# Two attention pipelines: values before the turn on TensorE, reading them out before the copy on VectorE, with a few edits around them

## The reference

```python
def diff_attend(q, k, v, lam):
    s = jnp.einsum('bqhmd,bkhmd->bhmqk', q, k).astype(jnp.float32) * (HEAD_DIM ** -0.5)
    p = jax.nn.softmax(s, axis=-1)
    w = p[:, :, 0] - lam * p[:, :, 1]
    return jnp.einsum('bhqk,bkhe->bqhe', w.astype(v.dtype), v)
```

## Time and profile before

| | |
|---|---|
| median of 3 runs | 2604.9 us (2600.58 to 2605.96) |
| profiled execution | 2598.19 us, of which its span 2596.4 us |
| TensorE, VectorE, ScalarE busy | 96%, 52%, 40% of the span |
| mean granted clock of TensorE | 0.987 of full |
| first attention pipeline (ab) | 1249 to 1366 us |
| second attention pipeline (cd) | 2270 to 2365 us |
| last product's end to span's end | 2587.5 to 2596.4 us |

### The profile page before, as it was taken

How to read it: one execution, slowest core, us unless ns; L and a number is a source line. 1 busy time by engine, 2 the same in 40 slices (tenths; PEclk the granted TensorE clock), 3 DMA queues, 4 the chain that set the end, 5 groups by cost and what they waited for, 6 DMA issues and landing times.

```text
span 2596.4 us, 37247 instructions
## 1 busy us (share of the span) xinstructions
PE 2490.1 (96%) x15710; PEld 2157.3 (83%) x15710; DVE 1350.2 (52%) x2245; ACT 1035.2 (40%) x1659; POOL 0.2 (0%) x4
## 2 busy tenths in 40 slices
PE   7999999999999999999789999999999999988998
PEld 6998789978997888888568888888888887868998
DVE  6657554655453334357886333335333347846554
ACT  5534544434433223146563322213222226744442
POOL 0000000000000000000000000000000000000000
PEclk9999999999999999999999999999999999999999
DMA  9886733488862333335102323332333326502554
GB/s 334 283 277 207 234 122 98 145 321 302 311 211 90 97 98 98 97 122 186 41 1 66 103 96 96 96 97 90 97 97 97 98 89 181 184 1 67 185 180 137
DMA packets 145639, 372.28 MB, mean 143 GB/s; under 512 B 20266, under 2 KB 65730, under 8 KB 145474
## 3 DMA queue, kind: packets, MB, share of 16 engines
q1 hardware_dynamic: 145186, 369.59, 44.0%
q10 hardware_dynamic: 288, 0.31, 0.1%
HBM read 368.71 MB, written 1.15 MB: 142 GB/s over the span
## 4 chain that ended last, share of the span: by engine, by line
PE 88%; DVE 7%; ACT 3%; issue 1%; DMA 1%; SPq 0%; ACTq 0%; DVEq 0%
PE psum L352 76%; PE psum L834 2%; PE psum L1701 2%; PE psum L1672 1%; DVE normed_raw L618 1%; DVE normed_lo L631 1%; PE psum L1689 1%; PE psum L1603 1%; PE psum L1291 1%; PE psum L1303 1%; DVE weights_lo L300 1%; DVE arena L1768 0%; ACT arena L1721 0%; PE psum L1166 0%; PE psum L1275 0%
## 5 line engine op out<-in xcount | busy, mean ns | idle before, releaser
L300 DVE TENSOR_TENSOR weights_lo<-weights_raw,weights_hi 128x1024 fp32r<-128x1024 f32 (+2 forms) x547 | 656.9, 1212 | 471.8 <-ACT weights_hi L294 469.0
L352 PE MATMUL psum<-normed_hi,weights_hi 128*128 128x256 f32 (+2 forms) x2664 | 880.6, 331 | 21.6 <-DVE normed_lo L631 6.8
L352 PE MATMUL psum<-normed_lo,weights_hi 128*128 128x256 f32 (+2 forms) x2664 | 866.7, 325 | 0.0
L352 PE MATMUL psum<-normed_hi,weights_lo 128*128 128x256 f32 (+2 forms) x2664 | 866.3, 325 | 0.0
L294 ACT CAST weights_hi<-weights_raw 128x1024 fp32r<-128x1024 f32 (+2 forms) x547 | 562.8, 1035 | 371.8 <-DMA weights_raw<-in_w_down 260.9
L352 PEld LDWEIGHTS psum<-normed_hi,weights_hi 128*128 128x128 f32 (+1 forms) x2664 | 508.6, 191 | 85.5 <-issue 35.1
L352 PEld LDWEIGHTS psum<-normed_lo,weights_hi 128*128 128x128 f32 (+1 forms) x2664 | 509.8, 191 | 41.5 <-issue 1.2
L352 PEld LDWEIGHTS psum<-normed_hi,weights_lo 128*128 128x128 f32 (+1 forms) x2664 | 509.6, 191 | 40.6
L352 PE MATMUL psum<-hidden_hi,weights_hi 128*128 128x512 f32 (+1 forms) x594 | 217.6, 366 | 0.0
L352 PE MATMUL psum<-hidden_hi,weights_lo 128*128 128x512 f32 (+1 forms) x594 | 217.1, 365 | 0.0
L352 PE MATMUL psum<-hidden_lo,weights_hi 128*128 128x512 f32 (+1 forms) x594 | 217.1, 365 | 0.0
(11 more groups left out here) (264 smaller groups left out, 2740.3 us busy)
## 6 DMA issues: line engine op xcount, KB each, us to landing
weights_raw<-in_w_gu SPq DMA_DIRECT2D x220, 512.0 KB, 3.6
weights_raw<-in_w_down SPq DMA_DIRECT2D x110, 512.0 KB, 3.6
arena<-in_w_mod SPq DMA_DIRECT2D x72, 512.0 KB, 6.9
weights_raw<-in_w_x SPq DMA_DIRECT2D x24, 512.0 KB, 6.5
resid<-in_w_mod SPq DMA_DIRECT2D x24, 512.0 KB, 7.5
normed_raw<-in_w_mod SPq DMA_DIRECT2D x24, 512.0 KB, 7.9
under_normed_hi<-in_w_mod SPq DMA_DIRECT2D x24, 512.0 KB, 7.7
weights_raw<-in_w_qk SPq DMA_DIRECT2D x24, 512.0 KB, 4.3
```

Source lines behind the costliest of these rows:

```text
L300: ve.tensor_tensor(w_lo[:, c % RING, a], w_raw[:, c % RING, a], w_hi[:, c % RING, a].bitcast(F32), ALU.subtract).then_inc(lo_ready, 1)
L352: last = te.matmul(out, a, b, start=start and n == 0, stop=stop and n == 2)
```

## The change

It has five parts.

1. In each step of `Attend` TensorE does the values of unit i-3 ahead of the turn of unit i-2 (before: behind it), and VectorE reads the values of unit i-3 out right behind the maxima, ahead of its copy for unit i-2 and the weights of unit i-1 (before: behind both). ScalarE's order is as it was.
2. In cd the side steps move: the last head norm from step 0 to step 1, the eight `Turns` steps from steps 1 to 4 to steps 2 to 5.
3. The end: `Turn` and `Store` and both meetings are gone. A stage `Output` transposes, copies and stores the result in five parts, the first three between the steps of the last product; the last two (blocks 6 and 7) stand behind it.
4. The last `IntoResid` adds up no squares (`sums=False`).
5. TensorE waits for the constants in `Modulation` only at its first transposition, no more at its first step.

```diff
@@ Attend
             def tensor(self, pe, i):
-                if 2 <= i < len(self.units) + 2:
-                    j, u = i - 2, self.units[i - 2]
-                    pe.wait_ge(*u.probs)
-                    if j >= 1:
-                        pe.wait_ge(aa_copied, self.base + j)
-                        pe.wait_ge(*self.units[j - 1].second)
...
-                    last.then_inc(aa_turned, 1)
                 if i >= 3:
                     j, u = i - 3, self.units[i - 3]
                     pe.wait_ge(aa_copied, self.base + j + 1)
...
                     last.then_inc(aa_pv, 1)
+                if 2 <= i < len(self.units) + 2:
+                    j, u = i - 2, self.units[i - 2]
+                    pe.wait_ge(*u.probs)
...
+                    last.then_inc(aa_turned, 1)
...
             def vector(self, dve, step, i):
                 if i < len(self.units):
                     self.maxima(dve, i)
-                if 2 <= i < len(self.units) + 2:
-                    j, u = i - 2, self.units[i - 2]
-                    if len(u.values) == 2:
-                        dve.wait_ge(aa_turned, self.base + j + 1)
-                        if j >= 2:
-                            dve.wait_ge(aa_pv, self.base + j - 1)
-                        w = len(u.values[1]) * P
-                        ve.tensor_copy(self.turned[:, j % 2, 1, 0:w], psum[:, 5, 0:w]).then_inc(aa_copied2, 1)
-                if 1 <= i <= len(self.units):
-                    self.weights(dve, step, i - 1)
                 if i >= 3:
                     j, u = i - 3, self.units[i - 3]
                     dve.wait_ge(aa_pv, self.base + j + 1)
...
                     last.then_inc(aa_out, 1)
+                if 2 <= i < len(self.units) + 2:
...
+                if 1 <= i <= len(self.units):
+                    self.weights(dve, step, i - 1)
@@ Modulation, tensor
                 if i == 0:
                     pe.wait_ge(cond_in, 1)
+                elif k < 0:
                     pe.wait_ge(const_in, 32)
-                elif k < 0:
                     pe.wait_ge(mod_rows, r)
...
+        class Output(Stage):
+
+            parts = ((0, 2), (2, 4), (4, 6), (6, 7), (7, 8))
...
+            def tensor(self, pe, i):
+                a, b = self.parts[i]
+                pe.wait_ge(*bank_free[self.down.group + b - 1])
+                for t in range(NT):
+                    for k in range(a, b):
+                        last = te.transpose(self.turned(i)[:, t, (k - a) * P:(k - a + 1) * P],
+                                            resid[:, k, t * P:(t + 1) * P], ident)
+                last.then_inc(out_mm, 1)
+
+            def scalar(self, act, step, i):
+                a, b = self.parts[i]
+                act.wait_ge(out_mm, i + 1)
+                se.copy(result[:, :, a * P:b * P], self.turned(i)).then_inc(out_copied, 1)
             def sync(self, sp, i):
...
+                a, b = self.parts[i]
+                sp.wait_ge(out_copied, i + 1)
+                sp.dma_start(out[0].rearrange("(t p) n -> p t n", p=P)[:, :, a * P:b * P],
+                             result[:, :, a * P:b * P]).then_inc(out_done, 16)
...
-        side = [(0, h_steps[24]), (0, h_steps[25])]
-        side += [(1 + n // 2, t_steps[18 + n]) for n in range(8)]
+        side = [(0, h_steps[24]), (1, h_steps[25])]
+        side += [(2 + n // 2, t_steps[18 + n]) for n in range(8)]
...
-        alone(*chain, norm, *ffn(W["w_gu21"], W["w_down21"], KF, TOK, hidden_x, (1, 8), [norm]))
...
+        up, down = ffn(W["w_gu21"], W["w_down21"], KF, TOK, hidden_x, (1, 8), [norm], sums=False)
+        output = steps_of(Output(down))
+        side = [((b * KF - 1) // CT + 2, step) for (_, b), step in zip(Output.parts, output)]
+        in_order(steps_of(*chain, norm, up), beside(steps_of(down), side))
```

More of the change, by code:

```diff
@@ L260, in build @@
         te, ve, se, ge = nc.tensor, nc.vector, nc.scalar, nc.gpsimd
[L262 removed]
+        counts = {"bias": 48, "normed": 0, "sums": 0, "norm_sum": 0,
                   "norm_av": 0, "norm_vv": 0, "hidden": 0, "heads": 0, "turns": 0, "turned_hi": 0, "pairs": 0, "joint": 0,
@@ L1704, in tensor @@
                     last.then_inc(aa_pv, 1)
+                if 2 <= i < len(self.units) + 2:
+                    j, u = i - 2, self.units[i - 2]
+                    pe.wait_ge(*u.probs)
+                    if j >= 1:
+                        pe.wait_ge(aa_copied, self.base + j)
+                        pe.wait_ge(*self.units[j - 1].second)
+                    for n in range(len(u.values)):
+                        for k in range(len(u.values[n])):
+                            last = te.transpose(psum[:, 4 + n, k * P:(k + 1) * P],
+                                                self.s[:, j % 3, n, k * P:(k + 1) * P], ident)
+                    last.then_inc(aa_turned, 1)
             def scalar(self, act, step, i):
@@ L1973, in mla_pairs, with __init__, turned, ffn @@
             return units
[L1975 to L1984 removed]
+        result = at(11264, NT, D)
+        out_mm, out_copied = sem("output_turned"), sem("output_copied")
+        class Output(Stage):
+            parts = ((0, 2), (2, 4), (4, 6), (6, 7), (7, 8))
+            n = len(parts)
+            def __init__(self, down):
+                self.down = down
+            def turned(self, i):
+                a, b = self.parts[i]
+                return psum[:, 3 + i, 0:NT * (b - a) * P].rearrange("p (t n) -> p t n", t=NT)
+            def tensor(self, pe, i):
[10 more added lines that the diff above has]
+                se.copy(result[:, :, a * P:b * P], self.turned(i)).then_inc(out_copied, 1)
+            def sync(self, sp, i):
+                a, b = self.parts[i]
+                sp.wait_ge(out_copied, i + 1)
+                sp.dma_start(out[0].rearrange("(t p) n -> p t n", p=P)[:, :, a * P:b * P],
+                             result[:, :, a * P:b * P]).then_inc(out_done, 16)
+                if i == self.n - 1:
+                    sp.wait_ge(out_done, 16 * self.n)
+        def ffn(up, down, tiles, a, pair, gate, norms, tail=None, sums=True):
             first = FfnUp(up, tiles, a, pair, norms)
[L1987 removed]
+            second = IntoResid(down, tiles, pair[1:], slice(0, a.stop - a.start), gate, sums=sums, tail=tail)
             second.ready = first.hidden_ready
@@ L2256, in _ @@
         def _(pe):
-            for steps, n in plan:
+            for steps in plan:
                 for stage, i in steps:
                     stage.tensor(pe, i)
-                meet(pe, n)
         @block.scalar
@@ L2264, in _ @@
             step = Steps(act, act_step)
-            for steps, n in plan:
+            for steps in plan:
                 for stage, i in steps:
                     stage.scalar(act, step, i)
-                meet(act, n)
         @block.vector
@@ L2272, in _ @@
             step = Steps(dve, dve_step)
-            for steps, n in plan:
+            for steps in plan:
                 for stage, i in steps:
                     stage.vector(dve, step, i)
-                meet(dve, n)
 def f_tiles(w):
```

72 lines of the change are left out of this document (16 added, 56 removed).

## The result

| | before | after |
|---|---|---|
| median of 12 runs | 2602.07 us (2595.81 to 2605.96) | 2614.15 us (2604.89 to 2626.99) |
| ratio | | 1.0046, 95% interval 1.0035 to 1.0058 |
| profiled execution, its span | 2598.19 us, 2596.4 us | 2613.69 us, 2611.9 us |

The account below looks back on a forecast made before the run. TensorE's work bounds the kernel outside a few stretches; in ab neither TensorE nor VectorE does throughout. Terms 6.7 (ab) + 2.1 (cd) - 2.4 (end) - 0.2 (start) = +6.2 us, on the 2604.9 median 2611.1 us; range 2602 to 2618.

Parts of the forecast that it names:

- Kind (a): Attention steps with VectorE full (5.83 of 6 us): TensorE gets earlier, VectorE takes no notice; taken at nothing.
- Kind (b): Attention steps with TensorE full: same instructions back to back, copy covered by the next scores; taken at nothing.
- Kind (c): Steps with engines waiting in a circle (side turns, SubNorm, ends): exponentials 1.7 to 1.9 us later; ab +6.7, bounds 2 and 9.
- a clock that would be better kept: ab steps 7 to 9: side turns and scores, 3 us, take 1.5 at full clock; low end 2.7 instead of 4.1.
- Steps 16 and 17: ab, SubNorm steps: TensorE arrives 0.9 us ahead, the circle costs 1.8; VectorE ready for next maxima 2.0 us later.
- Steps 24 to 26: ab steps 24 and 25: same shift with 256 keys, values being 8 matmuls instead of 16; 1.2 us.
- cd: Second side turn waits 10.1 instead of 9.4 us; step 6 scores 1.3 later, end 0.8; together +2.1, bounds -1 and 5.
- The end.: After the last product 3.9 us saved, store landing in 2.9; transposes add 1.5 within it; net -2.4, bounds -3.9 and -1.3.
- The start.: First matmul earlier, but full queues keep the modulation chunk at 33.0 us; -0.2, bounds -3.8 and +1.5.
- The low clock: Rival: waits at ab steps 7-9 and cd steps 2-5 each lose 1.5 us more at four places; +12.2, 2617.1; chance 0.14.
- "Faster": Rival: TensorE's 21.3 us of weight waits are on the path, 8 us fall away; -5.6, 2599.3 us; chance 0.09.
- "Start kept": Rival: the early constants' wait keeps its 3.8 us at the start; sum +2.6, 2607.5 us; chance 0.05.

Follow-up runs that it names:

- the end alone: Kernel before with only the new end (parts 3 and 4): 2599.66 us, ratio 0.9989.
- new in circles: Changed kernel with the new order only in 22 steps (ab 7-10, 16-18, 24-26, 32-34; cd 1-6, 16-18), old order elsewhere: 2617.59 us, 1.0063.
- the kernel with exponentials first: Kernel before with the new order on TensorE and VectorE, and ScalarE's exponentials of unit i ahead of its copy of unit i-2: 2620.92 us, 1.0077.
- old in circles: Changed kernel with the old order in ab 7-10, 16-18, 24-26, closing three, and cd 1-6, closing three; new order elsewhere: 2599.83 us, 0.9986.
- the order alone: Kernel before with only part 1, the new order on TensorE and VectorE in the attention steps: 2620.17 us, ratio 1.0067.
- all but the order: Changed kernel with the old order in the attention steps, parts 2 to 5 kept: 2595.73 us, ratio 0.9976.
- the early start alone: Kernel before with only part 5, TensorE's wait for the constants moved to Modulation's first transposition: 2602.32 us, ratio 0.9997.
- old order with exponentials first: Kernel before with only ScalarE's exponentials of unit i put ahead of its copy of unit i-2: 2618.82 us, ratio 1.0066.

## Why the prediction was right in direction and half in size

**Kind (a), VectorE full: taken at 0, measured about 2 us.** ab steps 0 to 6, 11 to 15 and 19 to 23 are longer by 1.1, 0.4 and 0.6 us. Six traces with the old order lie within 0.3 us of each other in the first of these stretches (22.2 to 22.5) and within 0.02 in the others, so this is more than chance. The step that failed is "VectorE, which is full, takes no notice": the new values wait for VectorE's readout of the values before, and the turn now stands behind them, so VectorE waits for the turn at its copy. In step 14 (2.98 us before, 4.04 after) the timeline of the changed kernel shows both:

```profile
1316.07 1.13 PE L1661 MATMUL psum<-arena 128*128 128x128 f32 x8 [0.97 <-DVE arena L1706]
...
1318.11 0.69 DVE L1718 COPY arena<-psum 128x512 f32<-128x512 f32 x1 [0.37 <-PE psum L1673]
```

Steps 11 to 13 gave back part of it.

**Kind (b), TensorE full: right in cd, with one exception in ab.** cd steps 7 to 14 take 35.9 us instead of 36.15; the chain of the changed kernel has scores, values and turn back to back:

```profile
2347.87 1.73 PE psum L1643 x8
2349.60 1.73 PE psum L1661 x16
2351.33 0.88 PE psum L1673 x8
```

The prediction said what it would cost if the next scores did not cover the copy, 0.2 to 0.7 us a step. Its cover was "scores of 1.06 to 2.12 us"; it left out the scores over 256 keys, which take 0.70 us. In ab steps 16 and 17 they stand over a copy of two halves, and each step takes 3.68 instead of 3.39 us, with a wait of 0.57 us of the values' weight load for the copy. (The prediction had counted these two steps under `SubNorm`, and so are they counted below.)

```profile
1322.74 1.86 PEld L1661 LDWEIGHTS psum<-arena 128*128 128x128 f32 x16 [0.57 <-ACT arena L1684]
```

**Kind (c) in ab, the mis-sized term.** Predicted for steps 7 to 9: 4.1 us less 1.4 for a clock that would be better kept. Steps 7 to 10 took 4.5 more. Two traces show these four steps nearly free of low clock, the end alone with the old order and new in circles with the new one:

```profile
1276.32:1298.66 22.34, 17.67 (x130) 13.47 (x129) 15.38 (x43) 11.91 (x30) 0.00 (x0) 1.00 0.00 1
```

```profile
1272.96:1299.08 26.12, 18.32 (x130) 13.76 (x129) 15.68 (x42) 11.27 (x28) 0.00 (x0) 0.97 0.00 1
```

That is 3.8 us more (0.3, 1.4 and 2.0 in steps 7, 8 and 10), 0.65 of it longer busy time of TensorE. So without low clock the shift is 3.1 to 3.8, against 4.1 predicted: it was sized well. What failed is the 1.4: it was not given back. The clock fell over values and turn instead: in step 8, which is 3.0 us longer, these two took 3.68 + 1.91 us instead of 1.90 + 1.04. Over the four steps TensorE is busy for 21.93 us instead of 19.08, which is 2.9 us of clock.

Steps 16 and 17 with 18, where their `SubNorm` work ends: predicted 2.0, measured 1.8, of it 0.6 by TensorE's longer busy time in step 18 (4.1 instead of 3.5 us). That the late copy of the turn is what delays the exponentials there is shown by the kernel with exponentials first, which takes the step 18 back to 4.20 us; what it costs elsewhere is in its experiment.

Steps 24 to 26: predicted 1.2, measured 1.3, but this match is luck. Steps 24 and 25, where the prediction had the shift, are 0.05 us longer each. Step 26 is longer by 1.2 us (6.25 instead of 5.03), and so it is with the old order in the end alone (6.19) and in old in circles (5.99). What differs is the clock under its values, here before, after, and in the end alone:

```profile
1342.35 1.08 PE L1701 MATMUL psum<-arena 128*128 128x64 f32 x8
```

```profile
1353.49 1.94 PE L1661 MATMUL psum<-arena 128*128 128x64 f32 x8 [2.40 <-DVE arena L1718]
```

```profile
1345.62 1.94 PE L1672 MATMUL psum<-arena 128*128 128x64 f32 x8
```

The end: predicted 0.8, measured 1.4 from step 27 on. From the scores of step 31 on it takes 13.7 us before, 14.9 with the change, 15.1 in new in circles and 14.1 in old in circles, so the closing steps cost some 1.2, and most of it goes with the old order there.

Taken together ab is 11.2 us longer instead of 6.7, and outside the bound of 9. Of the 4.5 us missing in the sum, 1.8 are the clock term with the wrong sign and its shift, 2.1 the full steps taken at nothing, 0.6 the end.

**cd.** Up to step 6 the change, with both edits, costs 1.25 us; I took 1.3. But these are two large terms, not two small ones. The four waits ahead of second side turns add up to 9.5 us before, 5.7 with the shift and the old order, 12.2 with the order alone, and 10.0 with both. So by the waits the shift gives 3.8 us, and the order behind it takes 4.2. By the lengths of steps 0 to 6 the shift gives 5 to 6 us against this trace of before and the order takes 6 to 7, but there the clock adds its chance: with the old order and the old list the same steps took 41.4, 43.9 and 44.4 us in three traces. By time the shift gives 2.6. The prediction gave it no gain, since it worked out only both together. The end of cd costs 2.2 us instead of 0.8 (1.7 in new in circles, where the clock stayed at 1.00): after each of the last turns the values wait 0.40, 0.83 and 0.83 us for copies, and the next product starts later.

**The end.** Predicted -2.4, measured -2.9 (-5.5 to -0.3) alone. The tail shrank by 5.2 us, not 3.9, mostly because the 128 KB store landed in 1.8 us, where the line through two larger loads gave 2.9. The Trainium skill ("DMA: Bandwidth & Descriptors", Anatomy of one DMA), with 2.3 by its fixed part, was nearer, and still high; that section describes transfers issued by GpSimd, and this store is issued by SyncE. The last two products were 3.1 us longer in the trace, for which I had 1.5. 1.8 us of them are the low clock at 2384 to 2392. That is not a debt of the order: 11 of the 14 traces have it at this place, five of them with the old order; the trace of before, at 1.00, is one of the three that don't. The window of all but the order there:

```profile
2363.00:2371.00 8.00, 8.00 (x56) 8.00 (x56) 3.72 (x6) 1.62 (x3) 0.00 (x0) 0.79 0.21 68
```

From cd to the last product's end that kernel takes 224.7 us.

**The start.** Predicted -0.2, measured alone -0.8 us (-3.6 to +1.8): full queues took the 3.8 us back. The bound of +1.5, that the idling costs clock, came true in part. In three of the five traces with edit 5 (the changed kernel, the early start alone, old in circles) the granted clock was 0.57 to 0.64 at 34 to 40 us; in the other two and in all nine traces without edit 5 it was 1.00. In these three the waits for the first chunk were 2.8 us or longer, in the other two 1.25 and 2.22. That this is why the first attention began 2.9 us later is not shown: without edit 5 it began anywhere from 1249.4 to 1254.0 us, and the times of twelve runs show no cost.

**The rivals.** The low clock, given 0.14 of the chances at 2617.1, describes the result as well as the forecast does: +12 is its number, and the trace has its mechanism in ab (7.1 of 11.2 us; an estimate that takes half of TensorE's busy time at a clock of 0.50 off leaves 87.3 us of busy time before and 87.5 after, so the clock is all of that difference). With the order alone the clock's part is larger still (13.1 of 14.3), with the new order in circles it is 6.1 of 6.7. Its places were not quite the predicted ones. In cd three of the four waits were followed by low clock (0.83 over each 10 us), the fourth, of 2.23 us as well, by none; and over steps 0 to 6 the mean clock was 0.89, against 0.88 before, so there it cost little more. The rule named beside it, a fall to half after idling, so agrees with the trace at most waits of 2 us and more, not at all of them. No kernel here kept the clock up throughout while leaving the order, so how much of the 12 us the clock alone would give back stays open; only in ab steps 7 to 10 does a pair of traces at nearly full clock exist, and there 3.1 to 3.8 us are left.

That the result of 2614.15 us lies well within the range owes something to two errors that offset each other: the change cost 5.9 us more than forecast, and the base, 2604.9 by three runs, was 2.8 us above the median of twelve.

"Faster" is refuted: the 21.3 us of waits for weights shrank to 3.9, and ab's steps with full VectorE got longer. Its sum was also wrong: difference units with 512 keys are 8, not 16, so it would have been 4 us, not 8. "Start kept" is refuted by the start alone.

## What to carry to other kernels

When one of three engines in a ring does its work earlier, list for each instruction that moved back (here the turn) who stands waiting in order behind its reader. Where traces at nearly full clock could be compared, that cost had been placed well (4.1 us for 3.1 to 3.8 in ab steps 7 to 10, waits of 10.1 for 10.0 in cd). What was not placed is the clock that falls behind such waits, and it was the larger part in ab. And a matching number proves little by itself: steps 24 to 26 matched for another reason, which a trace with the old order shows. A step in which an engine is full is not free of cost: a new wait ahead of an instruction that the full engine needs drains it. And a change of several edits is worth measuring by parts even if its sum is small: here parts of -6 and +17 us stood behind +12.

## What the runs showed of the hardware that I had not expected

TensorE's clock stayed at half for 19 us although the engine hardly idled. In the old order with exponentials first, from 1341 to 1360:

```profile
1341.00:1353.00 12.00, 11.90 (x51) 9.52 (x51) 5.99 (x25) 4.57 (x17) 0.00 (x0) 0.50 0.00 1
1353.00:1360.00 7.00, 7.00 (x30) 5.25 (x30) 5.68 (x18) 3.57 (x13) 0.00 (x0) 0.50 0.00 1
```

Start and length are followed by busy times and the clock as before. The page counts TensorE busy for 18.9 of 19 us at a granted clock of 0.50, that is 1.2 GHz; the same steps ran at 1.00 in the kernel before, at 6.59 busy of 7 us. At half clock the work of these steps fills the step, so each of them takes as long as TensorE needs. The clock is back at 1.00 in 1362 to 1364, where TensorE is busy for 1.80 of 2 us, and so before the next long gap; what raised it the traces do not show. The Trainium skill ("TensorE: Matmul & The Clock Gate", Part 1) has sustained activity release the clock; here 18.9 us of it did not.

The changed kernel's own runs spread over 22 us, and the spread goes with the mean granted clock: spans of 2603.1 us at 0.985 and of 2625.2 us at 0.975, for the same program.

A store of 128 KB landed in 1.8 us and one of 256 KB in 3.4, behind chunk loads, nearly the 3.6 and 3.7 of the 512 KB loads in the same stretch.
